# FFN weights of a hybrid encoder layer: cast during the scans into a bf16 copy in DRAM, loaded in bulk later

## The reference, cut to what matters

```
x = x + gate1 * mix                                   # mix: attention heads and mLSTM heads, then w_out
hff = rms_norm(x, g_norm2) * (1.0 + scale2) + shift2
gte, up = jnp.split(hff @ w_ffn_in, 2, axis=-1)       # w_ffn_in: 1024 x 5632 float32
ff = (jax.nn.silu(gte) * up) @ w_ffn_out              # w_ffn_out: 2816 x 1024 float32
return x + gate2 * ff                                 # gate2 depends on the sequence, not on the weights
```

## Time and profile before

| What | Value |
|---|---|
| Median of 3 runs | 2243.08 us |
| The profiled execution | 2236.5 us |
| Its span, slowest of 8 cores | 2235.0 us (2225.1 to 2235.0) |
| Segment 1 | 0 to about 165 us |
| Slot passes | about 200 to 735 us |
| Pass F, pass B | to about 1185 us, to 1416 us |
| Mixing stage | 1416 to 1700 us |
| FFN, with its start | 1700 to 2235 us |

### The profile page before, as it was taken

One profiled execution on the slowest core, in us unless ns is written; L12 is line 12 of the kernel. 1 busy time (PEld: TensorE's weight loads), 2 busy tenths in 40 slices (PEclk: granted clock), 3 DMA queues, 4 the chain that ended last, 5 costly groups with the idle time before them and its releaser, 6 DMA issues.

```text
span 2235.0 us, 37930 instructions; the slowest of 8 cores (2225.1 to 2235.0 us)
## 1 busy us (share of the span) xinstructions
PE 1508.9 (68%) x10986; PEld 1017.9 (46%) x11072; DVE 1012.4 (45%) x1904; ACT 952.8 (43%) x2004; POOL 823.5 (37%) x706
## 2 busy tenths in 40 slices
PE   4753666666666777777756766244443999999998
PEld 1322344434434555555545545111112777766665
DVE  0113565656555666666657776332442222322222
ACT  0004666656657566665666665123112222222211
POOL 0006566565566555565664442111332001111100
PEclk9886786877778999999788778566766999999999
DMA  8972111111111111110111100598872000111100
GB/s 263 315 241 85 57 57 58 57 57 57 48 60 55 55 60 51 44 44 34 62 44 37 53 29 20 170 304 276 275 223 106 20 29 29 39 39 39 39 20 20
DMA packets 79098, 199.66 MB, mean 89 GB/s; under 512 B 9392, under 2 KB 13488, under 8 KB 78768
## 3 DMA queue, kind: packets, MB, share of 16 engines
q1 hardware_dynamic: 78896, 197.24, 26.9%
HBM read 163.66 MB, written 33.55 MB: 88 GB/s over the span
## 4 chain that ended last, share of the span: by engine, by line
PE 47%; issue 11%; DMA 11%; ACT 11%; DVE 10%; POOL 7%; SPq 3%; DVEq 0%; ACTq 0%; POOLq 0%; another core or an unknown queue 0%
PE psum L1213 14%; PE psum L629 8%; PE psum L620 7%; PE psum L1229 7%; DMA arena<-w_fi 3%; DMA arena<-w_mod 3%; PE psum L1140 2%; SPq L386 2%; DMA arena<-w_fo 2%; ACT arena L946 2%; POOL arena L600 2%; PE psum L608 2%; DVE arena L651 2%; DMA arena<-w_main 1%; POOL arena L695 1%
## 5 line engine op out<-in xcount | busy, mean ns | idle before, releaser
L620 PE MATMUL psum<-arena 128*128 128x258 bf16 (+1 forms) x2048 | 322.1, 304 | 76.4 <-ACT arena L757 12.0
L1213 PE MATMUL psum<-arena 128*128 128x256 bf16 x2816 | 316.3, 276 | 21.4 <-ACT arena L1204 21.4
L582 POOL TENSOR_TENSOR arena<-arena 128x1 f32<-128x1 f32 (+1 forms) x154 | 102.7, 668 | 566.7 <-DVE arena L580 530.3
L1213 PEld LDWEIGHTS psum<-arena 128*128 128x128 bf16 x2816 | 278.7, 99 | 58.1 <-issue 22.6
L629 PE MATMUL psum<-arena 128*128 128x512 bf16 (+1 forms) x849 | 232.6, 423 | 91.1 <-ACT arena L649 28.8
L620 PEld LDWEIGHTS psum<-arena 128*128 128x128 bf16 x2048 | 208.3, 108 | 141.0 <-issue 99.8
L600 POOL TENSOR_TENSOR arena<-arena 128x1024 bf16<-128x1024 f32 x90 | 213.0, 2367 | 121.2 <-DVE arena L598 90.4
L651 DVE SCALAR_TENSOR_TENSOR arena<-arena 128x256 bf16<-128x256 f32 x224 | 188.4, 842 | 116.2 <-ACT arena L649 98.8
L629 PEld LDWEIGHTS psum<-arena 128*128 128x128 bf16 x912 | 90.1, 111 | 188.9 <-issue 145.2
L1219 DVE TENSOR_TENSOR arena<-psum,arena 128x256 bf16<-128x256 f32 x176 | 74.7, 424 | 223.1 <-PE psum L1213 153.9
L1218 ACT ACTIVATE arena<-psum 128x256 f32<-128x256 f32 x176 | 67.4, 383 | 235.5 <-PE psum L1213 227.3
(11 more groups left out here) (136 smaller groups left out, 2472.0 us busy)
## 6 DMA issues: line engine op xcount, KB each, us to landing
arena<-xp SPq DMA_DIRECT2D x106, 512.0 KB, 3.7
arena<-w_mod SPq DMA_DIRECT2D x12, 2048.0 KB, 18.9
arena<-w_fi SPq DMA_DIRECT2D x64, 352.0 KB, 5.8
arena<-w_main SPq DMA_DIRECT2D x16, 736.0 KB, 13.6
arena<-w_fo SPq DMA_DIRECT2D x44, 256.0 KB, 5.2
x_s<-arena SPq DMA_DIRECT2D x16, 512.0 KB, 4.7
arena<-x_s SPq DMA_DIRECT2D x16, 512.0 KB, 3.3
out<-arena SPq DMA_DIRECT2D x16, 512.0 KB, 2.6
```

Source lines behind the costliest of these rows:

```text
L620: P.op("pe", lambda e, kc=kc: e.matmul(pt.ap[:, 0:n], lhsT=Wb.ap[:, kc, col0:col0 + 128], rhs=hp.ap[:, kc, off:off + n], start=(kc == 0), ...
L1213: P.op("pe", lambda e, kc=kc, pt=pt, half=half, col=col: e.matmul(pt.ap[:, half * 256:(half + 1) * 256], lhsT=Wfi.ap[:, kc, col:col + 128] ...
```

## The change

The FFN weights are read, cast and written back to DRAM as bf16 during the scans, and read from there later.

- A new generator `gen_W` has 132 jobs: 88 blocks of `w_ffn_in` and 44 of `w_ffn_out`, 128 x 512 each. A job is a load (256 KB) into `wst_ring` (two buffers), a cast on POOL (with a cost of 1.3 in the planner) into `wbf_ring` (two buffers), and a store (128 KB) to `wfi_d` or `wfo_d`. In the program a job comes every seven steps, and `take(gw, 24)` adds 24 steps to every group of the scans, 40 groups in all.
- `do_wjobs`, its 108 loads and its casts are gone from the mixing stage. Behind `p2_loads(0)` stand eight DMAs that load `Wfi` from `wfi_d`, 128 x 5632 bf16 each. They are joined at the end of the stage.
- `Wfo` is loaded by four DMAs at the start of the FFN segment, in the program ahead of the loads of x1. It is joined in the first group ahead of the matmuls at L1229.
- gate2 is no longer part of the weights. L1233 becomes a product of PSUM and gate2 on DVE, and a new POOL operation adds x1.
- The sum of squares at L1190 writes into `hm` and no longer into a tile of its own.
- The planner's `WINDOW` is 160 and no longer 400, in all segments.

```diff
-    WINDOW = 400
+    WINDOW = 160
...
+        wst_ring = [A.tile([128, 512], F32, "wst%d" % i) for i in range(2)]
+        wbf_ring = [A.tile([128, 512], BF16, "wbf%d" % i) for i in range(2)]
+        wchunk = {}
+        wjobs_bg = [("fi", kc, c0) for kc in range(8) for c0 in range(0, 2 * DFF, 512)] + \
+                   [("fo", f, c0) for f in range(NFC) for c0 in (0, 512)]
+
+        def gen_W():
+            for j, (kind, a, c0) in enumerate(wjobs_bg):
+                src = (wfiv if kind == "fi" else wfov)[:, a, c0:c0 + 512]
+                dst = (wfi_d if kind == "fi" else wfo_d)[a * 128:(a + 1) * 128, c0:c0 + 512]
+                stt_, bft_ = wst_ring[j % 2], wbf_ring[j % 2]
+                load(stt_, src)
+                P.op("pool", lambda e, stt_=stt_, bft_=bft_: e.tensor_copy(out=bft_.ap, in_=stt_.ap), reads=[stt_], writes=[bft_], c=1.3)
+                b = Buf("wch%d" % j)
+                wchunk.setdefault((kind, a), []).append(b)
+                store(dst, b, bft_)
+                for _ in range(7):
+                    yield
...
+                streams.append(take(gw, 24))
                 interleave(streams)
...
-        interleave([objs[4]["B"](7)])
+        interleave([objs[4]["B"](7), gw])
...
-        gate2_p = A.tile([128, D], F32, "gate2p")
-        load(gate2_p, mod_s[1], rd=[mod_sb[1]])
...
         p2_loads(0)
+        Wfi.cast_bufs = []
+        for kc in range(8):
+            b = Buf("wfiL%d" % kc)
+            Wfi.cast_bufs.append(b)
+            P.op("sp", lambda e, kc=kc: e.dma_start(out=Wfi.ap[:, kc, :], in_=wfi_d[kc * 128:(kc + 1) * 128, :]),
+                 reads=wchunk[("fi", kc)], writes=[b], dma=True, c=8.0)
         for c in range(NT):
             if c + 1 < NT:
                 p2_loads(c + 1)
-            do_wjobs(7)
...
-        do_wjobs(1000)
         join(Wfi)
-        join(Wfo)
...
+        gate2_p = A.tile([128, D], F32, "gate2p")
+        load(gate2_p, mod_s[1], rd=[mod_sb[1]])
+        Wfo.cast_bufs = []
+        wfo_dv = wfo_d.rearrange("(f p) n -> p f n", p=128)
+        for f0 in range(0, NFC, 6):
+            f1 = min(f0 + 6, NFC)
+            b = Buf("wfoL%d" % f0)
+            Wfo.cast_bufs.append(b)
+            rds = [x_ for f in range(f0, f1) for x_ in wchunk[("fo", f)]]
+            P.op("sp", lambda e, f0=f0, f1=f1: e.dma_start(out=Wfo.ap[:, f0:f1, :], in_=wfo_dv[:, f0:f1, :]),
+                 reads=rds, writes=[b], dma=True, c=8.0)
...
-                P.op("act", lambda e, xt=xt, st=st: e.activation(out=junk_holder[0].ap, in_=xt.ap, func=AF.Square, accum_out=st.ap[:, 0:1]),
-                     reads=[xt], writes=[junk_holder[0], st])
+                hm = hm_ring[i % 2]
+                P.op("act", lambda e, xt=xt, st=st, hm=hm: e.activation(out=hm.ap, in_=xt.ap, func=AF.Square, accum_out=st.ap[:, 0:1]),
+                     reads=[xt], writes=[hm, st])
...
-                    P.op("dve", lambda e, pt=pt, half=half, xt=xt, x2=x2: e.tensor_tensor(out=x2.ap[:, half * 512:(half + 1) * 512], in0=pt.ap,
-                                                                                        in1=xt.ap[:, half * 512:(half + 1) * 512], op=ALU.add),
-                         reads=pb + [xt], writes=[x2])
+                    hs_ = slice(half * 512, (half + 1) * 512)
+                    P.op("dve", lambda e, pt=pt, hs_=hs_, x2=x2: e.tensor_tensor(out=x2.ap[:, hs_], in0=pt.ap, in1=gate2_p.ap[:, hs_], op=ALU.mult),
+                         reads=pb + [gate2_p], writes=[x2])
                     pfree(pt)
+                    P.op("pool", lambda e, hs_=hs_, xt=xt, x2=x2: e.tensor_tensor(out=x2.ap[:, hs_], in0=x2.ap[:, hs_], in1=xt.ap[:, hs_], op=ALU.add),
+                         reads=[x2, xt], writes=[x2])
```

More of the change, by code:

```diff
@@ L322, in build_program @@
     x1_s = nc.dram_tensor("x1_s", [NT, 128, D], F32).ap()
+    wfi_d = nc.dram_tensor("wfi_d", [D, 2 * DFF], BF16).ap()
+    wfo_d = nc.dram_tensor("wfo_d", [DFF, D], BF16).ap()
     hf_b = [Buf("hf%d" % i) for i in range(NT)]
@@ L1018, in gT, with take @@
             return chain(*[objs[p]["T"](e_) for e_ in es if e_ <= 17])
+        wfiv = w_fi.rearrange("(kc p) n -> p kc n", p=128)
+        wfov = w_fo.rearrange("(f p) n -> p f n", p=128)
+        wst_ring = [A.tile([128, 512], F32, "wst%d" % i) for i in range(2)]
[15 more added lines that the diff above has]
+                    yield
+        def take(g_, n):
+            for _ in range(n):
+                try:
+                    next(g_)
+                except StopIteration:
+                    return
+                yield
+        gw = gen_W()
         interleave([gT(0, range(5))])
@@ L1072, in build_program @@
         junk2 = A.tile([128, 128], BF16, "junk2")
[L1073 to L1092, removed]
         def p2_loads(c):
@@ L1161, in build_program @@
         x1_ring = [A.tile([128, D], F32, "x1l%d" % i) for i in range(4)]
-        junk3 = A.tile([128, D], BF16, "junk3")
+        gate2_p = A.tile([128, D], F32, "gate2p")
[9 more added lines that the diff above has]
+                 reads=rds, writes=[b], dma=True, c=8.0)
         t1_ring[:] = [A.tile([128, D], F32, "t1b%d" % i) for i in range(1)]
@@ L1171, in build_program @@
         st3_ring = [A.tile([128, 4], F32, "st3_%d" % i) for i in range(2)]
-        junk_holder = [junk3]
         def ffn_loads(gi):
@@ L1195, in ffn_group @@
                                                                                 op0=ALU.mult, op1=ALU.mult), reads=[xt, st, A2_p], writes=[t1])
-                hm = hm_ring[i % 2]
                 P.op("pool", lambda e, t1=t1, hm=hm: e.tensor_tensor(out=hm.ap, in0=t1.ap, in1=B2_p.ap, op=ALU.add),
@@ L1221, in ffn_group @@
                 pfree(pt)
+            if gi == 0:
+                join(Wfo)
             for t in range(2):
```

## The result

The changed kernel takes 2259.96 us, the median of ten runs (2257.43 to 2264.05), against 2243.61 us for the kernel before in as many runs. The ratio is 1.0082, with a 95% interval of 1.0070 to 1.0094: 0.8% slower, 16.4 us. Two of the ten runs before (2336.72 and 2342.83 us) were in a slower state of the chip and do not enter the ratio. The profiled execution's span is 2257.2 us (before 2235.0).

What follows compares the result with a forecast made beforehand. No engine is full: engines' waits on each other set the scans, DMA the mixing stage, PE the FFN. 18 - 29 + 21 + 1 = +11 us on 2236.5 gives 2247.5; the run median, 6.6 higher, 2254, range 2215 to 2300.

Steps and rivals of the forecast that it cites:

- Scans, the jobs: Scans: 132 added casts, with their effect on DVE, lengthen them by 18 us, bounds 0 and 93.
- the cast work itself: Scans: of 81 us of POOL casts, 19% is on the path, 15 us.
- The DVE term: Scans: added POOL work stretches DVE's L651 by 12 us in all, of which 3 us reach the end.
- Scans, the order: Scans: the planner's window of 160 makes new orders, taken as zero, with 26 us to either side.
- order worse: Rival, scans: the shorter window orders them worse, time 2280; chance 0.10.
- Waits in order: Rival, scans: casts wait for loads held on SP, so 18 us becomes 81, time 2317; chance 0.15.
- Mixing stage: Start 38 us later behind eight bulk loads, 15 tile periods of 11.2 us save 67; together -29 us.
- The rival on PE's clock: Mixing stage: denser work keeps PE at 2.4 GHz, saving 29 us over 15 tiles, time 2225; chance 0.08.
- overtaken: Rival, mixing stage: x and w_out pieces overtake the bulk loads, no 38 us delay, time 2216; chance 0.04.
- FFN's start: Start of the FFN: Wfo's loads and gate2, 6.29 MB ahead of x1's loads, cost 21 us.
- FFN: FFN: only the last added POOL addition is on the path, +1.3 us, bounds 1.0 and 1.6.

Runs made afterwards that it cites:

- cast_tiny: Changed kernel with all casts but the first two 8 columns wide, still waiting for full loads; ratio 1.0072 to the kernel before, scans 1289.9 us.
- cast_no_wait: Changed kernel with casts reading an always-present tile, so POOL waits for no weight load; ratio 1.0045 to the kernel before, scans 1283.1 us.
- jobs_ahead: Changed kernel's order, but the 132 jobs lifted into one block ahead of the scans; scans 1282.2 us, ratio 1.1472 to the kernel before.
- woven: Changed kernel with scans planned without the jobs, which are then put into POOL's planned gaps; ratio 0.9921 to the kernel before, scans 1261.1 us.
- window_400: Changed kernel with the planner's window back at 400; ratio 1.0043 to the kernel before, scans 1292.1 us.
- wfi_spread: Changed kernel with Wfi's eight loads issued one each behind the mixing stage's first eight tiles; ratio 0.9908 to the kernel before.
- jobs_in_slots: Changed kernel with all 132 jobs in the three slot passes, 40 steps a group; ratio 1.0247 to the kernel before, scans 1333.8 us.
- pool_add_before: Kernel before with only L1233's sum split into a DVE copy from PSUM and a POOL addition; ratio 0.9930, FFN 496.5 us.

## Why the prediction was right in its number, and what in it was wrong

The forecast was 2254 us, +11; the kernel took 2259.96, +16.4. Two steps were wrong and offset each other in part. In the two profiled executions the scans came out 29 us above the forecast's +18, the FFN 15 us below its +1, the mixing stage 4.5 us below its -29, and together they grew by 22.2 us, twice the forecast. That the time still lies near 2254 is in part luck.

- **Scans, the jobs: +18.** Near. They cost 11 us in the new order and 13 in the old one. The way there was not that of the prediction: the cast work itself, for which 15 us stood, gave 3 us (`cast_tiny`), and the waits for loads, for which nothing stood, gave 10 (`cast_no_wait`; 6 by the mean of eight cores). The casts' 609 ns median is the 612 that was worked out from the earlier trace rows. The DVE term was too large. L653's mean fell from 842 to 786 ns with 74 us more of POOL work in the scans (748 us over the first three windows, 675 in the earlier trace rows), but that fall is the order's: `jobs_ahead`, in the new order and with no cast beside the scans, has 782 ns. With the order held, the casts lengthen the operation by 4 ns in the new order (782 to 786) and by 19 in the old one (842 to 861 in `woven`). Over 224 operations that is 1 to 4 us of DVE time, where the prediction had 12 and let 3 of them reach the end.
- **Scans, the order: 0, bounds ±26.** This is the step that failed. The order costs 34 us (`jobs_ahead`), beyond the bound. "I take zero, and an eighth of it, 26 us, to either side" had no row behind the eighth. And it was put under the window, which does nothing (`window_400`); what makes the order anew is that the jobs are in the list that the planner works on. The last sentence of the prediction had named this as the way to be wrong: the scans' length moved by more than 30 us. The rival "order worse" with its chance of 0.10 had the right sign, the wrong source and too small a price.
- **Waits in order: a rival with 63 us.** The waits exist, 59 us of idle POOL time, and they cost 6 to 10.
- **Mixing stage: +38 and -67.** Measured +30.6 and -64.1. The mechanism was right in both; the eight loads at 334 GB/s and not 300 take 34.5 us, which is 3.5 us of the 7.4 at the start; the rest is not traced. The working on the start misread one row: the hb_s load at 1438.27 is the fourth, the third is issued at 1433.51; no number hung on it. The period is 11.4 us and not 11.2, and PE's clock rose from 0.68 to 0.71 only. The rival on PE's clock did not come: in the changed kernel's last two tiles 16 matmuls take 5.37 and 5.09 us, 336 and 318 ns each (in the last tiles of `wfi_spread` 305 to 345), where the faster rate is 220. The rival "overtaken" is refuted by the 36.92 us wait.
- **FFN's start: +21.** Measured +20.0.
- **FFN: +1.3.** Measured -13.4. The prediction priced the work of the POOL addition and not its effect on ACT's order. It is the same oversight as in the scans, with the other sign.

Open is why the new order of the scans is 34 us worse: the two orders differ in hundreds of places, and no single one was found or tried.

## What to carry to other kernels

When a planner with estimated costs orders all engines, an operation added to its list can make every engine's order in that segment anew, and that can cost more than the operation: price it by planning, and keep background work out of the plan and put it into the gaps of the finished one. Here the plan itself gave a warning. `_schedule`, run without a chip, ends the segment with the scans at 994 us for the kernel before, at 1044 for the changed one and at 1105 for `jobs_in_slots`: +50 and +111, where the chip gave +47 and +92. It is no measure of everything: for `pool_add_before` it ends the FFN segment 1 us earlier, and the chip took 14 us less.

A bulk load belongs behind everything that starts the next stage, the tiles which an engine's in-order list reads soon after included; ask of each moved load what stands behind it in the queue. And before a loss or gain is put down to the work that was moved, look at the stages that only had their order changed.

## What the runs showed of the hardware that had not been expected

- A PE wait of 2.87 us at the start of an FFN group goes with 352 matmuls that take 40.25 us in every second group from the third on; with a wait of 1.30 us all groups but the first take 38.59 us. In the first 4.42 us of the third group the granted clock is 0.62, between the levels of 1.2 and 2.4 GHz; in the same stretch of the fourth it is 1.00, the level of 2.4 GHz, although both groups had the same wait. Why only every second one falls is open. Over the FFN the granted clock is 0.98 in the one kernel and 0.99 in the other.
- Full DMA engines on a core moved 334 GB/s from 1478 to 1515 us, mostly for `Wfi`'s rows of 11 KB of bf16, more than the 318 in the float32 loads of segment 1.
- A DVE operation's mean time changed more with the order of the engines' lists than with the sum of POOL's work: L651 took 842 ns in the kernel before and 861 in `woven`, which has all 132 casts more in the same order; in the new order it took 782 without casts beside it (`jobs_ahead`) and 786 with them.
